# Expert rounds with the tokens held still: weights move 512 columns at a time, and five of the rounds are written out

## The reference

```python
def moe_swiglu(h, router, w_gu, w_down):
    hf = h.reshape(B * T, D)                       # 640 tokens in all
    logits = (hf @ router).astype(jnp.float32)     # 8 experts
    top_v, top_i = lax.top_k(logits, TOP_K)        # TOP_K = 2
    wts = jax.nn.softmax(top_v, axis=-1)
    gate = jnp.sum(jax.nn.one_hot(top_i, N_EXP) * wts[..., None], axis=-2)
    g, u = jnp.split(jnp.einsum('nd,edf->nef', hf, w_gu), 2, axis=-1)   # D_FF_E = 1408
    act = jax.nn.silu(g) * u * gate[..., None]
    return jnp.einsum('nef,efd->nd', act, w_down)
```

## Time and profile before

| | |
|---|---|
| median of 3 runs | 2706.48 us (2704.94 to 2707.95) |
| profiled execution, span | 2713.9 us |
| TensorE busy over the span | 88% |
| VectorE, ScalarE busy over the span | 53%, 39% |
| expert rounds, in the profiled execution | 8, from 1893.4 us to about 2657 us |
| mean busy share of the DMA engines in the rounds | 0.67 |

### The profile page before, as it was taken

One profiled execution on the slowest core, in us unless ns is written; L12 is line 12 of the kernel. 1 busy time (PEld: TensorE's weight loads), 2 busy tenths in 40 slices (PEclk: granted clock), 3 DMA queues, 4 the chain that ended last, 5 costly groups with the idle time before them and its releaser, 6 DMA issues. The chain is left out here.

```text
span 2713.9 us, 47159 instructions
## 1 busy us (share of the span) xinstructions
PE 2386.3 (88%) x19349; PEld 2177.9 (80%) x19349; DVE 1444.5 (53%) x2038; ACT 1069.2 (39%) x1753; POOL 335.3 (12%) x347
## 2 busy tenths in 40 slices
PE   5996687888899999989967788895999999999993
PEld 4985465778899999989845667794999999999992
DVE  5577556774422222245665667743555555555556
ACT  4332136673422112143321366633444444444443
POOL 0055333001000000000553330012000000000002
PEclk8998899999899999989988999997999999999996
DMA  5332764703122322222127200025676676567664
GB/s 209 94 85 45 203 209 160 248 1 94 47 78 59 90 78 63 59 57 87 56 53 205 90 6 1 1 63 194 181 231 204 181 230 207 173 196 238 196 183 163
DMA packets 453116, 340.49 MB, mean 125 GB/s; under 512 B 90961, under 2 KB 421151, under 8 KB 451935
## 3 DMA queue, kind: packets, MB, share of 16 engines
q1 hardware_dynamic: 436383, 277.43, 35.2%
q10 hardware_dynamic: 11520, 41.95, 4.8%
q0 software_dynamic: 5056, 18.88, 1.8%
HBM read 287.68 MB, written 50.53 MB: 125 GB/s over the span
## 5 line engine op out<-in xcount | busy, mean ns | idle before, releaser
L2360 PE MATMUL ps<-h_hi,w_hi 128*128 128x256 f32 x1408 | 399.5, 284 | 1.6 <-DVE h_lo L2506 1.6
L2360 PE MATMUL ps<-h_hi,w_lo 128*128 128x256 f32 x1408 | 399.0, 283 | 0.0
L2360 PE MATMUL ps<-h_lo,w_hi 128*128 128x256 f32 x1408 | 399.0, 283 | 0.0
L2514 DVE TENSOR_TENSOR w_lo<-w_raw,w_hi 128x2048 fp32r<-128x2048 f32 (+1 forms) x180 | 309.1, 1756 | 119.0 <-ACT w_hi L2409 119.0
L2360 PEld LDWEIGHTS ps<-h_hi,w_hi 128*128 128x128 f32 x1408 | 270.6, 192 | 4.7 <-issue 2.0
L2360 PEld LDWEIGHTS ps<-h_lo,w_hi 128*128 128x128 f32 x1408 | 270.7, 192 | 2.8
L2360 PEld LDWEIGHTS ps<-h_hi,w_lo 128*128 128x128 f32 x1408 | 270.6, 192 | 0.0
L2409 ACT CAST w_hi<-w_raw 128x2048 fp32r<-128x2048 f32 (+1 forms) x180 | 256.4, 1474 | 0.1
L2747 PE MATMUL ps<-ffn_h_hi,w_hi_ffn 128*128 128x320 f32 x704 | 161.9, 311 | 5.5 <-DVE ffn_h_lo L378 4.2
L2421 ACT ACTIVATE tokens_then_blocks<-ps 128x256 f32<-128x256 f32 x88 | 33.8, 384 | 325.8 <-PE ps L2360 325.7
L2747 PE MATMUL ps<-ffn_h_lo,w_hi_ffn 128*128 128x320 f32 x704 | 161.3, 311 | 0.0
(11 more groups left out here) (447 smaller groups left out, 5478.0 us busy)
## 6 DMA issues: line engine op xcount, KB each, us to landing
w_raw<-in_moe_w_gu SPq DMA_DIRECT2D x182, 512.0 KB, 5.1
w_raw<-in_moe_w_down SPq DMA_DIRECT2D x91, 512.0 KB, 5.9
G_decay<-in_ada_w ACTq DMA_DIRECT2D x54, 512.0 KB, 4.7
w_ahead<-in_ffn_w_gu SPq DMA_DIRECT2D x44, 512.0 KB, 5.3
slots_h<-tm SPq DMA_DIRECT2D x13, 1024.0 KB, 11.2
slots_y<-tm SPq DMA_DIRECT2D x12, 1024.0 KB, 11.3
w_ahead<-in_ffn_w_down SPq DMA_DIRECT2D x16, 704.0 KB, 4.7
oA<-in_ada_w ACTq DMA_DIRECT2D x20, 512.0 KB, 5.5
```

Source lines behind the costliest of these rows:

```text
L2360: mm = pe.matmul(ps[:, j % 2, half * BLK:(half + 1) * BLK], gu(wt, j, half, k), x[:, k, :], start=(k == 0 and n == 0), stop=(k == KC - 1 a ...
L2514: dve.tensor_tensor(wlo[:, q, part], raw[:, q, part], whi[:, q, part].bitcast(F32), ALU.subtract).then_inc(s["lo_d" if down else "lo_u"], 1)
```

## The change

Names that are new: a **unit** u (six of them, NU) is 256 inner columns, the last one 128. A **tile** is 128 of the block's 256 tokens. `multiply(r, u, tile)` computes gate and up of one unit for one tile with the tokens held still and the weights moving: 24 products of 512 columns (256 gate, 256 up), in the last unit of 256. Its result has the tokens on the partitions, so `turn_act` turns the activations (two transposes of 128x128 per tile, one in the last unit) before the down product can use them. The weights come in 17 **pieces** (ORDER) of 2048 columns instead of 11 chunks of 3072: for each unit two gate/up pieces ("g", four of the eight D-chunks each) and one down piece ("d"). There are six raw slots, five slots each for hi and lo. The first two pieces are loaded early; the other four of the first round wait until the tokens are turned (`h_tok`), because h_moe now lies in the raw slots. VectorE's slot computation orders the experts by count. Rounds 0 to 4 (STATIC) are written out; the others are a loop of the same `work(r)`. All rounds have 256 slots (SIZES); branches for 128 and 192 exist but none of them is taken.

```diff
+STATIC = 5
+RMAX = NE + 5
...
+        NU, PW, SMALL = 6, 2048, 64
+        ORDER = [("g", 0, 0), ("g", 0, 1), ("g", 1, 0), ("g", 1, 1), ("d", 0, 0)]
+        for u in range(2, NU):
+            ORDER += [("g", u, a) for a in range(2 if u < NU - 1 else 1)] + [("d", u - 1, 0)]
+        ORDER += [("d", NU - 1, 0)]
+        RAW, HL = 6, 5
+        hl_before = [max([m - NP for m in range(NP) if m % HL == n % HL] + [m for m in range(n) if m % HL == n % HL]) for n in range(NP)]
...
+            SIZES = (256, 256, 256, 256, 256)
+            REGION = (0, 3, 1, 4, 2)
...
+            def wait_used(eng, r, n):
...
+                kind, u, _ = ORDER[n]
+                if kind == "g":
+                    eng.wait_ge(s["gu"], unit_done(r, u))
+                else:
+                    eng.wait_ge(s["dn"], count("units", r, u + 1))
...
-                    for j in range(SL):
-                        load_w(0, j)
+                    for n in range(2):
+                        load_w(0, n)
+                    sp.wait_ge(s["h_tok"], 2 * NT)
+                    for n in range(2, RAW):
+                        load_w(0, n)
...
+                        for k in range(KC):
+                            if k == 0 or k == 4 and u < NU - 1:
+                                pe.wait_ge(s["w_lo"], count("pieces", r, at("g", u, k // 4) + 1))
+                            for n, (x, wt) in enumerate(((hhi, whi), (hhi, wlo), (hlo, whi))):
+                                mm = pe.matmul(ps[:, bank, 0:2 * columns(u)], x[:, k, tile * P:(tile + 1) * P], gate_up(wt, u, k),
+                                               start=(k == 0 and n == 0), stop=(k == KC - 1 and n == 2))
+                        mm.then_inc(s["gu"], 1)
+
+                    def turn_act(r, u, tile):
...
+                        pe.wait_ge(s["prod"], tile_count(r, u, tile))
...
+                            for b in range(blocks_of(u)):
+                                mm = pe.transpose(ps[:, 2, 256 * tile + b * P:256 * tile + (b + 1) * P], act_tok[:, tile, b * P:(b + 1) * P],
+                                                  self.ident)
...
+                    def work(r):
...
+                        for u in range(NU):
+                            for tile in order:
+                                multiply(r, u, tile)
+                            for tile in order[:-1]:
+                                turn_act(r, u, tile)
+                            if u:
+                                down(r, u - 1, 0)
+                                if c == 256:
+                                    down(r, u - 1, 1)
+                            turn_act(r, u, order[-1])
+                            if u == NU - 3:
+                                pe.wait_ge(s["blk_in"], count("blocks", r, PER["blocks"][next_size(r)], 1))
+                                turn_group(coming[0])
+                            if u == NU - 1:
+                                for n, g in enumerate(coming[1:]):
+                                    if n == 2:
+                                        pe.wait_ge(s["h_lo"], count("groups", r, 1, 1))
+                                    turn_group(g)
+                        for tile in range(len(order)):
+                            down(r, NU - 1, tile)
+                    for r in range(STATIC):
+                        work(r)
                     with pe.Fori(0, rounds) as r:
...
+                        work(r)
```

That was TensorE's program; this is ScalarE's, and VectorE's has the same order:

```diff
+                    def work(r):
...
+                        for u in range(NU - 1):
+                            gate(r, u, order[0])
+                            split(r, 3 * u + 2)
+                            for tile in order[1:]:
+                                gate(r, u, tile)
+                            take(r, u, order[0])
+                            split(r, 3 * u + 3)
+                            for tile in order[1:]:
+                                take(r, u, tile)
+                            split(r, 3 * u + 4)
+                        for tile in order:
+                            gate(r, NU - 1, tile)
+                        upper(r, next_size(r), 0, 1)
+                        for tile in order:
+                            take(r, NU - 1, tile)
+                        for m in range(1, coming):
+                            upper(r, next_size(r), m, 1)
+                        for n in range(2):
+                            split(r, n, 1)
+                        act.wait_ge(s["dn"], count("units", r, NU))
```

More of the change, by code:

```diff
@@ new lines, in down @@
+                    def down(r, u, tile):
+                        c = size(r)
+                        pe.wait_ge(s["a_lo"], unit_done(r, u))
+                        pe.wait_ge(s["w_lo"], count("pieces", r, at("d", u) + 1))
+                        if u == 0 and not is_first(r):
+                            pe.wait_ge(s["y_act"], count("rounds", r))
+                            pe.wait_ge(s["y_dve"], count("rounds", r))
+                        for b in range(blocks_of(u)):
+                            st, sp_ = u == 0 and b == 0, u == NU - 1 and b == blocks_of(u) - 1
+                            if few(c, tile):
+                                for half in range(2):
+                                    mm = pe.matmul(ps[64 * half:64 * half + 64, 6, :], a_few[:, u % 2, b], down_rows_raw(u, b, half),
+                                                   start=st, stop=sp_)
+                                continue
@@ new lines, in _, with split, gate @@
+                    rounds = act.value_load(meta[0:1, RMAX + 1:RMAX + 2], min_val=1, max_val=RMAX - STATIC)
+                    def split(r, n, ahead=0):
+                        q = raw_slot[n]
+                        act.wait_ge(s[f"raw{q}"], count_raw(q, r, per_round[q] * ahead + landed[n]))
+                        wait_used(act, r, hl_before[n] + NP * ahead)
+                        act.copy(part(whi, n), raw_piece(n)).then_inc(s["w_hi"], 1)
+                    def gate(r, u, tile):
+                        c = size(r)
+                        wd = columns(u) // 2 if few(c, tile) else columns(u)
+                        act.wait_ge(s["gu"], tile_count(r, u, tile))
+                        act.activation(act_tok[:, tile, 0:wd], ps[:, gate_bank(c, u, tile), 0:wd], ACT.Silu).then_inc(s["silu"], 1)
@@ new lines, in take, with upper @@
+                    def take(r, u, tile):
+                        c = size(r)
+                        if few(c, tile):
+                            return
+                        act.wait_ge(s["a_turned"], tile_count(r, u, tile))
+                        if not (is_first(r) and u < 2):
+                            act.wait_ge(s["dn"], count("units", r, u - 1))
+                        act.copy(act_place(ahi, u, tile), act_turned(c, u, tile)).then_inc(s["a_hi"], 1)
+                    def upper(r, c, m, ahead):
+                        g = groups(c)[m]
+                        if g[1] is None:
+                            return
+                        act.wait_ge(s["h_turned"], count("groups", r, m + 1, ahead))
+                        act.copy(group_place(hhi, g), turned_group(g)).then_inc(s["h_hi"], 1)
@@ new lines, in split, with gate @@
+                    def split(r, n, ahead=0):
+                        dve.wait_ge(s["w_hi"], count("pieces", r, NP * ahead + n + 1))
+                        dve.tensor_tensor(part(wlo, n), raw_piece(n), part(whi, n).bitcast(F32), ALU.subtract).then_inc(s["w_lo"], 1)
+                    def gate(r, u, tile):
+                        c = size(r)
+                        wd = columns(u) // 2 if few(c, tile) else columns(u)
+                        dve.wait_ge(s["silu"], tile_count(r, u, tile))
+                        dve.tensor_tensor(act_tok[:, tile, 0:wd], act_tok[:, tile, 0:wd], ps[:, gate_bank(c, u, tile), wd:2 * wd], ALU.mult
+                                          ).then_inc(s["prod"], 1)
```

564 lines of the change are left out of this document (362 added, 202 removed).

## The result

| | before | changed |
|---|---|---|
| median | 2707.22 us (2704.94 to 2715.0, 4 runs) | 2746.14 us (2742.15 to 2753.36, 4 runs) |
| profiled execution: span, own time | 2713.9, 2715.0 us | 2746.6, 2748.27 us |
| first expert product to last pair | 1893.42 to 2656.71: 763.3 us | 1898.71 to 2688.85: 790.1 us |
| store to store | 95.3 us | 99.1 us |

The changed kernel takes 1.0127 times as long, 95% interval 1.0099 to 1.0156: slower, as forecast, and 1 us from the 2745 us predicted. The medians differ by 38.9 us and the two profiled executions by 32.7; the forecast difference was 38.5.

What follows compares the result with a forecast made beforehand. TensorE was taken as the bound, busy for all 95.3 us of a round. Terms 1 + 16 + 17 + 4 + 0.5 = 38.5 us on 2706.5 gave 2745 us, 1.4% slower; range 2728 to 2768, stretched to 2720 to 2772.

Steps and rivals of the forecast that it cites:

- TensorE's own work: In the rounds: fewer, wider products save 2.6 us, new transposes cost 2.7; +1 us in all, between -5 and +7.
- unit 0: First unit of each round: TensorE waits 0.85 us before turning tile 1 and 1.2 for piece 3; +16 us, 13 to 24.
- seams: Between rounds: TensorE waits 2.4 us for piece 0, split behind the token casts; seven times, +17 us, 13 to 22.
- start: Before the rounds: longer slot computation, scatter sharing DMA with early weight pieces, less disturbed issue, earlier first products; +4 us.
- end, to the last store: After the last round: its result is copied behind two casts and two w_lo; +0.5 us.
- Rival 5: Gate/up products: the fixed part goes altogether, 0.213 us per 512 columns, 31 us less in all, 2714 us; chance 0.03.
- t: In unit 0: the time at which multiply(0, 1) has issued its last product.
- Contention: Before the rounds: early weight pieces share the DMA engines with the scatter; 0 to 7.6 us, middle 4 taken.
- rival 1: At the new waits in seams and unit 0, TensorE's clock falls; 2756 to 2790 us, say 2765; chance 0.10.
- Rivals 2 to 4: The last of these: more than eight rounds, a ninth costing 99 us, 2844 us; chance 0.01.
- Rival 2: Seams and unit 0: waits are covered, only the saving stays; 2690 us, chance 0.04; with transposes paid 2712, chance 0.03.
- Rival 3: In the written-out rounds: longer code starves TensorE, 1% of five rounds, +5 us, 2750 us; chance 0.03.

Runs made afterwards that it cites:

- e8: e7 with piece 1 kept in buffer 2 and piece 2 in buffer 1; 2704.47 us, ratio 0.9965 to the kernel before.
- e1: Changed kernel with tile 1's activations of unit 0 turned inside unit 1, behind its first tile; 2767.88 us, one execution.
- e2: Changed kernel with piece 3 split before tile 1's Silu and product in unit 0; 2760.66 us, one execution.
- e3: Changed kernel with the edits of e1 and e2 together; 2744.46 us, ratio 1.0109 to the kernel before.
- e4: Changed kernel with piece 0 in buffer 4, split right behind the first token group at the seam; 2746.77 us, ratio 1.0113 to the kernel before.
- e5: Changed kernel with the first round's pieces 2 to 5 loaded after the scatter and the first token block; 2739.73 us, one execution.
- e9: The changed kernel again, unaltered, on another chip; 2748.52 us, ratio 1.0137 to the kernel before.
- e10: The kernel of e1 again, timed on the same chip as e9; 2764.37 us, ratio 1.0197 to the kernel before.
- e6: Changed kernel with one round written out and seven in the loop, instead of five and three; 2767.88 us, one execution.
- e7: Changed kernel with the edits of e3, e4 and e5 together; 2719.98 us, ratio 1.0030 to the kernel before.
- e11: The kernel of e2 again, timed on the same chip as e9; 2746.53 us, ratio 1.0126 to the kernel before.

## Why the prediction was right

The direction, the size and the places of the waits were right; how the cost of unit 0 is made up was not, and the nearness to 1 us is luck. Term by term, in us over the kernel, against the profiled difference of 32.7:

| step of the prediction | predicted | measured | how |
|---|---|---|---|
| TensorE's own work | +1 | -4.6 | 8 x (94.73 - 95.3), e8 |
| unit 0 | +16 | +14.4 | 8 x (1.30 + 0.50) |
| seams | +17 | +16.7 | 7 x 2.39 |
| start | +4 | +5.3 | 1898.71 - 1893.42 |
| end, to the last store | +0.5 | +0.2 | 6.84 - 6.61 behind the last pair |
| sum | 38.5 | 32.0 | 0.7 left over |

**TensorE's own work** is where the sum was off most. Two sizes were taken from rows that stood nearest and were a little high: the 512-column gate/up products run at 0.227, below the 0.229 of the down pairs (0.55 us a round), and the transposes cost 0.21 a pair and not 0.25. The bounds given, -5 to +7, just hold it. The -4.6 is read from e8, where nothing waits; the changed kernel's own rounds less their three waits are 99.13 - 4.19 = 94.94, mostly because the second product behind each wait for w_lo starts 0.31 to 0.33 us after the first and not 0.227. The exchange of operands does save what its diff suggests, some 5 us in eight rounds; the 31 us that waits cost around it hide that. Rival 5 (0.213) is not borne out. The Trainium skill's gap (TensorE: Matmul & The Clock Gate, "Back-to-back issue gap"), N/2.4 + 2.5 ns or 216 ns, which the page gives for an isolated product, is not what this stream shows either: 227 ns.

**Unit 0.** The sum was right (1.80 for 2.05) and its split was not. The prediction added a wait of 0.85 for the product of tile 1 and one of 1.2 for piece 3. Measured are 1.30 and 0.50, and the first ends with VectorE's act_lo of tile 0, not with that product, which is done at t + 1.03 as forecast. The helper `turn_act` waits for both, and the second wait is one that the prediction did not read in the code:

```python
pe.wait_ge(s["prod"], tile_count(r, u, tile))
if not (is_first(r) and u == 0 and tile == tiles_of(c)[0]):
    pe.wait_ge(s["a_lo"], tiles_before(r, u, tile))
```

No run took that wait away alone. The sum came out right because both waits run against one deadline, piece 3's lower half at about t + 5.0 (2311.19 - 2306.17, forecast 5.25); whatever is waited before it is not waited at it. e1, e2 and e3 show that: take away either and the other grows, take away both and 1.9 us go. The prediction also has a table load of 1.3 us before each round's first Silu, as before; the changed kernel has it once, at 1899.4 us, and no term rested on it.

**The seam** was right to 0.01 us, and for the reason given: piece 0 behind three token casts. What the prediction missed is what stood behind it. It called piece 1's wait for down(5) no wait, true only behind a late piece 0; e4 paid for that.

**The start.** Slots +2.0 (+2.3 predicted) and the less disturbed issue on GpSimd -1.2 (-1.3) are right. Contention was 6.3 us (the scatter landed at 1889.9 where 1883.6 follows from the other two; 6.1 by e5), not the middle value 4: I split a range of 0 to 7.6 although no row was near its middle. Turns between the queues, as the Trainium skill has it (DMA: Bandwidth & Descriptors, "Queues, rings and completion order"), would have given +7, and the queue rows with 47.5% and 46.9% agree with it. The first products were 1.7 us closer behind the scatter, not 0.8.

**The clock**, rival 1, was given 0.10 on the ground that an idle of 1.75 us left the clock at 1.00. In the profiled execution it did not occur. e9 and e10 show that this ground was too weak and the mechanism real: idles of 2.24 and 1.90 us lie where the clock sometimes falls, and a fall costs 1.6 to 1.8 us, the low end of the 1.5 to 3 that the rival had. The median of the changed kernel lies 39 (36 in e9) and not 33 us above the one before. Such falls in other executions could explain the rest, and so could the plain scatter of executions, 10 to 11 us from the fastest to the slowest of each kernel; neither is shown. e10 is what rival 1 had described: its ratio of 1.0197 is 2760 us on the first comparison's scale, where the rival had 2765.

**Rivals 2 to 4.** Rival 2's condition, piece 0's lower half within down(5), had to be built by hand, in e4, and the other waits cleared with it, in e8; then the time is indeed below the kernel before, by 9 us where the rival had said 16 at most. Rival 3, code that starves TensorE, is excluded for the rounds by e6 and e8, and so is a loss or gain at a loop's branch of more than 0.2 us. There were eight rounds.

## What to carry to other kernels

Price an exchange of operands first in the busy engine's own time, then walk the in-order programs of the engines that feed it and ask of each tile when its last input is ready: here 5 us of saving met 31 us of waits at two places where the cover had been moved away. Waits in series towards one deadline do not add and do not go one by one; list all inputs of that deadline and clear them together, with the next one behind them (piece 1 here) already checked. A piece's buffer is part of its schedule: two buffer numbers were worth 14 us between e7 and e8 (7 x 2.0).

## What the runs showed of the hardware

- The granted clock can fall to 0.50 behind an idle of 2.24 us of TensorE, and behind one of 1.90, in a stage with TensorE otherwise 96% busy: products 0.43 us apart for about 3.5 us, 1.6 to 1.8 us lost each time. Behind the same 2.24 us it stayed at 1.00 in all seven seams of the changed kernel's first profile. How often it fell differed between kernels (none to three of seven seams with the changed kernel's rounds; five or six in e3, e1 and e10) and between executions of one kernel (four in e2, one in e11).
- An indirect scatter of 5.24 MB lands 18.8 us after its first issue without weight loads behind it (e5, e7, e8) and 24.9 to 25.5 us beside four pieces of weights, 4.2 MB (nine traces), with the DMA engines shared almost evenly, 47.5% to 46.9% (after).
- Products of 512 columns whose held operand changes in two of three steps (h_hi, h_hi, h_lo) run 0.227 us apart, no slower than the down pairs that share one (0.229).
- A loop's branch costs TensorE nothing that shows: looped and written-out rounds are both 94.7 us in e8, where nothing waits; the one in which the loop is entered is 94.9.
